# An encoder layer on one core: layer weights kept in two parts in DRAM for the second sequence, every second small part of the u tiles made anew by GpSimd

## The chip, the core and the metric

The kernel runs on 1 core of one Trainium2 chip, with its five engines: TensorE (PE; its weight loads are the row PEld), VectorE (DVE), ScalarE (ACT), GpSimd (POOL) and SyncE (SP), which here only issues DMAs. The metric is device time in microseconds of one execution. Three runs of the kernel before took 3474.37, 3475.89 and 3476.72 us; the median is 3475.89 us.

## The reference

One encoder layer (depth 1) is run on two sequences of 512 tokens with 1024 features, "prompt" and "sample", with the same weights. All is float32.

```
x = layer_norm(x)
h = x @ w_in                       # f_in 512, q 512, k 128, v 128, two gates of 1024
f = fft over tokens and group features of f_in, real part;  a = window attention(q, k, v)
x = layer_norm(2**0.25 * x + (sigmoid(g1) * (f @ w_fo) + sigmoid(g2) * (a @ w_ao)) @ w_out)
# PEER: 8 heads, 2 x 128 keys, the 16 best of 16384 experts for each token and head
eidx, gate = top16(x @ w_q, keys);  act = gelu(x . u[eidx])
cm  = sum(gate * act * v[eidx])
out = layer_norm(2**0.25 * x + cm + sigmoid(x @ ple_wg) * (p @ ple_wp))
```

## The kernel before

**Two parts.** A product that needs float32 accuracy is made of three TensorE matmuls (lines 1198 to 1200): large part by large part, large by small, small by large. The large part of a tile (w_hi) is a rounded copy that ScalarE makes (split_w, L464, for layer weights; split_u, L615, for u). The small part (w_lo for layer weights, u_lo for u) is raw minus large, on GpSimd, in two halves of 512 columns (split, L716).

**Tiles.** A layer has 69 weight tiles of 128x1024 (512 KB): 11 for the Fourier input, q, k and v, 24 for gates and merge (MERGE_AT), 8 for w_out (OUT_AT), 16 for w_q (QUERY_AT), 10 for the ple term (PLE_AT). Then come 128 u tiles. Each of these tiles is 24 matmuls with 512 columns. After the 128 u tiles of the sample come 128 v tiles (24 matmuls each), for the sample alone.

**Order.** Prompt: layer, u tiles (all expert activations, each tile of them stored to act_dram; VectorE chooses the experts beside it). Sample: layer, u tiles 0 to 61 (VectorE chooses, four choices of 128 tokens, and TensorE turns each choice at tiles CHOICE_AT = 16, 31, 46, 61), u tiles 62 to 125 with one batch of gates each (8 extra small matmuls, each in the trace as two, on one-hot tiles that VectorE makes, spread_batch), two more u tiles, then the v tiles.

**The prompt's experts.** The prompt's weighted sum over v goes by gather instead: 512 rows (4 token tiles by 128 choices), each an indirect DMA of 128x1024 from v into v_row (L767, 4 buffers) and an indirect DMA of 128 activations (L750, "value"), both issued by GpSimd in fetch_rows; VectorE adds each row into acc (L861) in add_rows. The rows are laid out over the whole sample part by fixed numbers: VectorE's are rows_before(j) at layer tile j, 2 at each of 10 gaps of a choice, 2 for each batch of gates, the rest over the v tiles (rows_at). A row can only be asked for when VectorE has taken the row four before (semaphore row_taken).

**Small parts of u.** In the prompt GpSimd makes all 128 and SyncE stores them to lo_dram; in the sample SyncE loads them back (u_lo_back), so GpSimd makes none. In the sample's layer GpSimd does both its 69 splits and rows, in the order that the loop over LAYER_TILES writes out: split of a tile, then the rows due. SyncE's queue loads weight j when the small part of tile j - 2 is made (load_w). In the v tiles VectorE makes the small parts.

## Time and profile before

| | |
|---|---|
| median of three runs | 3475.89 us |
| profiled execution | 3475.6 us, its span 3473.8 us |
| TensorE busy | 3240.2 us, 93% |
| VectorE busy | 1972.3 us, 57% |
| GpSimd busy | 2047.1 us, 59% |
| ScalarE busy | 1093.1 us, 31% |
| mean granted TensorE clock | 0.972 |
| GpSimd rows and values (L767, L750), 512 each | 691.9 us and 633.0 us |
| GpSimd splits of layer weights, 276 halves | 355.3 us |
| GpSimd splits of u, 256 halves | 362.1 us |

The profile is of one execution, and a busy TensorE is not one at its peak: matmuls overlap, so the number of matmuls in a stretch says more than the busy time. The chain of work that ended last has 67% of the span on TensorE and 17% on GpSimd. The shares of the page mix stages; a stage is read from the windows of the trace, and a wait by what ended it.

### The profile page before, as it was taken

The numbers are of one execution on the slowest core, as the hardware profiler recorded it, in microseconds if no ns is written. First come the engines' busy times: TensorE is split into PE (matmuls) and PEld (weight loads), VectorE is DVE, ScalarE is ACT, GpSimd is POOL, SyncE is SP. The second block draws the span as 40 slices with busy tenths as digits, with TensorE's granted clock in tenths as the row PEclk, the third lists the DMA queues.
The fourth block names the chain that finished last, engine by engine and source line by source line (L and its number), as shares of the span: only waits on it lengthen the run. The fifth ranks groups of instructions, "written<-read, shape, count | busy, mean of one in ns | idle before, by whom it ended". The sixth has DMA issues, their size and how long they took to land.

```text
span 3473.8 us, 40747 instructions
## 1 busy us (share of the span) xinstructions
PE 3240.2 (93%) x14740; PEld 2654.7 (76%) x14740; DVE 1972.3 (57%) x3363; ACT 1093.1 (31%) x1496; POOL 2047.1 (59%) x1568
## 2 busy tenths in 40 slices
PE   7999899999999999787889999999997999999997
PEld 6588787888888875566778888788886777777775
DVE  3511318992000007323437999788885877787778
ACT  2522223333222235211222333344453222222221
POOL 3044345565444474566476556577775888788883
PEclk9999899999999999888899999999998999999998
DMA  4022237777777853444349999899999999999995
GB/s 162 17 90 97 79 102 252 242 240 242 241 241 242 266 183 119 153 143 146 113 154 351 372 365 367 315 398 394 395 392 389 318 337 342 333 334 338 328 333 201
DMA packets 302660, 879.73 MB, mean 253 GB/s; under 512 B 44688, under 2 KB 77968, under 8 KB 299920
## 3 DMA queue, kind: packets, MB, share of 16 engines
q1 hardware_dynamic: 211216, 604.46, 49.9%
q0 software_dynamic: 91264, 272.96, 22.0%
q8 instruction: 103, 1.69, 0.2%
q14 instruction: 77, 0.63, 0.1%
HBM read 701.11 MB, written 176.16 MB: 253 GB/s over the span
## 4 chain that ended last, share of the span: by engine, by line
PE 67%; POOL 17%; issue 5%; DVE 5%; DMA 3%; ACT 1%; DVEq 1%; SPq 0%; POOLq 0%; ACTq 0%
PE ps L1198 20%; PE ps L1200 20%; PE ps L1199 20%; POOL value L750 8%; POOL v_row L767 8%; PE ps L1446 3%; DMA v_row<-in_v_rows,row_i 2%; POOL w_lo L716 1%; DVE acc L861 1%; PE ps L1376 1%; PE ps L1297 1%; DMA w_raw<-in_weights 1%; ACT probs L531 1%; PE ps L1339 0%; PE ps L1282 0%
## 5 line engine op out<-in xcount | busy, mean ns | idle before, releaser
L1198 PE MATMUL ps<-xt_hi,w_hi 128*128 128x512 f32 (+1 forms) x2800 | 1140.8, 407 | 63.9 <-POOL w_lo L716 53.1
L1199 PE MATMUL ps<-xt_lo,w_hi 128*128 128x512 f32 (+1 forms) x2800 | 1089.3, 389 | 0.0
L767 POOL DMA_INDIRECT v_row<-in_v_rows,row_i x512 | 691.9, 1351 | 502.2 <-DVE acc L861 396.7
L1200 PE MATMUL ps<-xt_hi,u_lo 128*128 128x512 f32 x2048 | 801.0, 391 | 0.0
L861 DVE SCALAR_TENSOR_TENSOR acc<-v_row,share,acc 128x1024 f32<-128x1024 f32 x512 | 663.1, 1295 | 190.9 <-DMA v_row<-in_v_rows,row_i 152.1
L750 POOL DMA_INDIRECT value<-act_dram,value_i x512 | 633.0, 1236 | 155.2 <-issue 154.9
L1198 PEld LDWEIGHTS ps<-xt_hi,w_hi 128*128 128x128 f32 x2800 | 537.0, 192 | 158.7 <-POOL w_lo L716 60.8
L1199 PEld LDWEIGHTS ps<-xt_lo,w_hi 128*128 128x128 f32 x2800 | 537.1, 192 | 84.2 <-issue 0.5
L716 POOL TENSOR_TENSOR w_lo<-w_raw,w_hi 128x512 fp32r<-128x512 f32 x276 | 355.3, 1310 | 388.6 <-ACT w_hi L464 387.6
L716 POOL TENSOR_TENSOR u_lo<-u_raw,w_hi 128x512 fp32r<-128x512 f32 x256 | 362.1, 1436 | 342.1 <-ACT w_hi L615 329.1
L1198 PE MATMUL ps<-w_hi,a_hi 128*128 128x512 f32 x1024 | 405.4, 396 | 61.0 <-DVE a_lo L1170 60.9
L634 ACT ACTIVATE act_t<-ps 128x512 f32<-128x512 f32 x256 | 153.1, 598 | 971.8 <-PE ps L1200 971.8
L1200 PEld LDWEIGHTS ps<-xt_hi,u_lo 128*128 128x128 f32 x2048 | 385.1, 188 | 82.3
L1200 PE MATMUL ps<-w_hi,a_lo 128*128 128x512 f32 x1024 | 403.2, 394 | 0.0
L1199 PE MATMUL ps<-u_lo,a_hi 128*128 128x512 f32 x1024 | 403.2, 394 | 0.0
L1200 PE MATMUL ps<-xt_hi,w_lo 128*128 128x512 f32 (+1 forms) x752 | 288.6, 384 | 0.0
L1198 PEld LDWEIGHTS ps<-w_hi,a_hi 128*128 128x128 f32 x1024 | 195.3, 191 | 111.6 <-DVE u_lo L1168 51.5
L615 ACT ACTIVATE w_hi<-u_raw 128x1024 fp32r<-128x1024 f32 x256 | 272.3, 1064 | 23.1 <-PE ps L1200 14.0
L827 DVE TENSOR_TENSOR xt_lo<-ps,xt_hi 128x512 fp32r<-128x512 f32 x32 | 20.4, 682 | 401.2 <-ACT xt_hi L474 401.2
L695 ACT ACTIVATE w_hi<-u_raw 128x1024 fp32r<-128x1024 f32 x128 | 135.6, 1059 | 336.0 <-PE ps L1200 335.9
L1446 PEld LDWEIGHTS ps<-hot_row,hot_col 128*128 128x128 f32 x1024 | 192.9, 188 | 44.9
L1200 PEld LDWEIGHTS ps<-w_hi,a_lo 128*128 128x128 f32 x1024 | 194.9, 190 | 41.3
(174 smaller groups left out, 3651.1 us busy)
## 6 DMA issues: line engine op xcount, KB each, us to landing
u_raw<-in_u_t SPq DMA_DIRECT2D x256, 512.0 KB, 6.4
w_raw<-in_weights SPq DMA_DIRECT2D x138, 512.0 KB, 3.3
lo_dram<-u_lo SPq DMA_DIRECT2D x128, 512.0 KB, 5.1
act_dram<-act_t SPq DMA_DIRECT2D x256, 256.0 KB, 5.2
u_lo<-lo_dram SPq DMA_DIRECT2D x128, 512.0 KB, 7.6
u_raw<-in_v_rows SPq DMA_DIRECT2D x128, 512.0 KB, 5.9
g_dram<-g_tile SPq DMA_DIRECT2D x16, 2048.0 KB, 13.2
act_in<-act_dram SPq DMA_DIRECT2D x128, 256.0 KB, 6.6
```

Of the source, the lines that this page charges most:

```text
L531: act.activation(probs[:, u % 2, h, 0:w], probs[:, u % 2, h, 0:w], ACT.Exp, bias=neg_max[:, u % 2, h:h + 1], accum_out=row_sum[:, u % 2, h ...
L615: act.activation(w_hi[:, (mu + n) % 2, :], u_raw[:, slot, :], ACT.Copy).then_inc(w_hi_made, 1)
L634: act.activation(act_t[:, slot, :], ps[:, n % 2, :], ACT.Gelu).then_inc(act_made, 1)
L695: act.activation(w_hi[:, n % 2, :], u_raw[:, n % DEEP, :], ACT.Copy).then_inc(v_hi_made, 1)
L716: pool.tensor_tensor(lo[:, here], raw[:, here], hi[:, here].bitcast(F32), ALU.subtract).then_inc(w_lo_made[half], 1)
L750: pool.indirect_dma_start(out=value[:, tt, k:k + 1], out_offset=None, in_=values, in_offset=bass.IndirectOffsetOnAxis(ap=value_i[:, tt, k: ...
L767: pool.indirect_dma_start(out=v_row[:, i % ROWS_DEEP, :], out_offset=None, in_=v_rows, in_offset=bass.IndirectOffsetOnAxis(ap=row_i[:, tt, ...
L861: dve.scalar_tensor_tensor(out=there, in0=v_row[:, i % ROWS_DEEP, :], scalar=share[:, tt, k:k + 1], in1=there, op0=ALU.mult, op1=ALU.add). ...
L1198: pe.matmul(where, lh, rh, start=first, stop=False)
L1199: pe.matmul(where, lh, rl, start=False, stop=False)
L1200: return pe.matmul(where, ll, rh, start=False, stop=last)
L1446: mm = pe.matmul(ps[:, 4 + 2 * (batch % 2) + k // 4, cols_of(k % 4)], hot_col[:, batch % 2, k, :], hot_row[:, batch % 2, k, :], start=True ...
```

## The change

Four things change.

1. **Pairs.** In the prompt's layer SyncE stores both parts of each tile to pair_dram (keep_w, 1 MB for each of 69 tiles, in two DMAs, queued behind the load of the tile two later). ScalarE may overwrite w_hi only once the tile is stored (w_kept). In the sample's layer SyncE loads both parts as one 1 MB DMA into one of three slots (load_pair), when TensorE has used the tile three before; ScalarE's and GpSimd's splits of the sample's layer are gone, and TensorE waits for pair_in.
2. **u tiles.** Only the small parts of even u tiles are stored in the prompt and loaded in the sample (64 of 128). In the sample GpSimd makes those of odd tiles (MADE), between the rows.
3. **Rows.** GpSimd asks first for 18 values, then rows_at_tile(n) rows ahead of the split of odd tile n. VectorE takes 10 rows before the first scores of the sample's attention, 16 in it, then 7 for every 4 layer tiles. By the end of the sample's layer 125 rows are due instead of 75; the choices (80) and batches (128) keep theirs, and the v tiles have 179 instead of 229.
4. **Loops.** TensorE's loops of the sample's layer are written out, since three slots don't fit a loop of two.

```diff
-LAYER_ROWS = 7
+START_ROWS, UNIT_ROWS = 10, 2
-FIRST_VALUES = 3
+FIRST_VALUES = 18
+PAIRS = 3
 def rows_before(j):
-    return j + LAYER_ROWS
+    return START_ROWS + UNITS * UNIT_ROWS + 7 * (j - MERGE_AT) // 4
+def reloaded(n):
+    return n % 2 == 0
+def rows_at_tile(n):
+    gates = n - GATES_AT
+    return ROWS_LAYER + GAPS * GAP_ROWS * NT * n // GATES_AT if gates < 0 else rows_at_batch(min(gates, GATE_BATCHES))
...
+        pair = at("pair", 42, [P, PAIRS, 2, D], F32R)
...
+            def keep_w(m):
+                slot = m % 2
+                sp.dma_start(pair_dram[m, :, 0, :], w_hi[:, slot, :].bitcast(F32)).then_inc(w_kept[slot], 16)
+                sp.dma_start(pair_dram[m, :, 1, :], w_lo[:, slot, :].bitcast(F32)).then_inc(w_kept[slot], 16)
+            def load_pair(j):
+                sp.dma_start(pair[:, j % PAIRS].bitcast(F32), pair_dram[j]).then_inc(pair_in[j % PAIRS], 16)
             def load_layer(s, first, last):
                 for j in range(first, last):
-                    load_w(s * STREAM + j, (s * STREAM + j) % 2, weights[j])
+                    if s:
+                        sp.wait_ge(w_used, made(STREAM + j - PAIRS))
+                        load_pair(j)
+                    else:
+                        load_w(j, j % 2, weights[j])
+                        if j >= 2:
+                            keep_w(j - 2)
...
                 if s == 0:
+                    for j in (LAYER_TILES - 2, LAYER_TILES - 1):
+                        sp.wait_ge(w_lo_made[1], made(j))
+                        keep_w(j)
...
-                        sp.dma_start(lo_dram[n], u_lo[n % DEEP][:].bitcast(F32)).then_inc(u_lo_stored[n % DEEP], 16)
+                        if reloaded(n):
+                            sp.dma_start(lo_dram[n], u_lo[n % DEEP][:].bitcast(F32)).then_inc(u_lo_stored[n % DEEP], 16)
...
                     for n in range(EXPERT_TILES):
-                        sp.wait_ge(w_hi_made, mu + n + 1)
+                        sp.wait_ge(w_hi_made, STREAM + n + 1)
+                        if not reloaded(n):
+                            sp.wait_ge(w_lo_made[1], 2 + STREAM + made_upto(n))
...
             def split_w(s, m, slot):
-                act.wait_ge(w_in[slot], landed(m - s * EXPERT_TILES, slot))
+                if s:
+                    return
+                act.wait_ge(w_in[slot], landed(m, slot))
+                act.wait_ge(w_kept[slot], 16 * (m - slot) + 16)
                 act.wait_ge(w_used, slot_free(m))
...
+                    if s == 0 and n < 2:
+                        for kept in range(2):
+                            act.wait_ge(w_kept[kept], 16 + 32 * len(range(kept, LAYER_TILES, 2)))
                     act.activation(w_hi[:, (mu + n) % 2, :], u_raw[:, slot, :], ACT.Copy).then_inc(w_hi_made, 1)
...
-            for j in range(LAYER_TILES):
-                m = STREAM + j
...
-                split_w(m, m % 2)
...
-                fetch_rows(rows_fetched(j))
+            for _ in range(FIRST_VALUES):
+                fetch_value()
+            pool.wait_ge(resid_stored, 16 * NT)
+            for tt in range(2):
+                fetch_acc(tt)
+            for n in MADE:
+                m = STREAM + LAYER_TILES + n
+                fetch_rows(rows_at_tile(n))
+                pool.wait_ge(w_hi_made, STREAM + n + 1)
+                split(u_lo[n % DEEP][:], w_hi[:, m % 2, :], u_raw[:, n % DEEP, :])
             fetch_rows(GATHERS)
...
+                if s:
+                    add_rows(START_ROWS)
                 dve.wait_ge(mix_in, 32 * (s + 1))
...
+            def arrived(s, m, half):
+                if s:
+                    pe.wait_ge(pair_in[(m - STREAM) % PAIRS], 16 * ((m - STREAM) // PAIRS + 1))
+                else:
+                    pe.wait_ge(w_lo_made[half], made(m))
...
-                pe.wait_ge(u_lo_back[slot], 16 * (n // DEEP + 1))
+                if reloaded(n):
+                    pe.wait_ge(u_lo_back[slot], 16 * (kept_before(n) + 1))
+                else:
+                    for half in range(2):
+                        pe.wait_ge(w_lo_made[half], 2 + STREAM + made_upto(n))
```

The order of GpSimd's instructions in the sample's layer, before (w_lo is the small part of a layer weight, v_row a gathered row, value a gathered activation; "waits" names semaphores):

```order
L716 TENSOR_TENSOR w_lo<-w_raw,w_hi 128x512 [waits w_hi_made]
L716 TENSOR_TENSOR w_lo<-w_raw,w_hi 128x512
L767 DMA v_row<-in_v_rows,row_i 128x1024 [waits row_taken]
L750 DMA value<-act_dram,value_i 128x1
L716 TENSOR_TENSOR w_lo<-w_raw,w_hi 128x512 [waits w_hi_made]
L716 TENSOR_TENSOR w_lo<-w_raw,w_hi 128x512
```

and now, from the last u tile of the prompt (u_lo_68 to u_lo_71 are the four slots of small parts) into the sample's layer:

```order
L778 TENSOR_TENSOR u_lo_70<-u_raw,w_hi 128x512
L778 TENSOR_TENSOR u_lo_71<-u_raw,w_hi 128x512 [waits w_hi_made]
L778 TENSOR_TENSOR u_lo_71<-u_raw,w_hi 128x512
L812 DMA value<-act_dram,value_i 128x1 [waits act_stored3,act_stored2,row_i_made,act_stored1,act_stored0]
L812 DMA value<-act_dram,value_i 128x1 x17
L798 DMA acc<-resid_dram 128x1024 [waits resid_stored]
L798 DMA acc<-resid_dram 128x1024
L829 DMA v_row<-in_v_rows,row_i 128x1024
L812 DMA value<-act_dram,value_i 128x1
```

The two halves of a split no longer stand behind a row that waits for row_taken; only values and rows are left there.

GpSimd at the end of the sample's layer and the start of the choices, before:

```order
L767 DMA v_row<-in_v_rows,row_i 128x1024 [waits row_taken]
L750 DMA value<-act_dram,value_i 128x1
L716 TENSOR_TENSOR w_lo<-w_raw,w_hi 128x512 [waits w_hi_made]
L716 TENSOR_TENSOR w_lo<-w_raw,w_hi 128x512
L767 DMA v_row<-in_v_rows,row_i 128x1024 [waits row_taken]
L750 DMA value<-act_dram,value_i 128x1
L767 DMA v_row<-in_v_rows,row_i 128x1024 [waits row_taken]
L750 DMA value<-act_dram,value_i 128x1
```

and now, at a place in the batches of gates:

```order
L829 DMA v_row<-in_v_rows,row_i 128x1024 [waits row_taken]
L812 DMA value<-act_dram,value_i 128x1
L829 DMA v_row<-in_v_rows,row_i 128x1024 [waits row_taken]
L812 DMA value<-act_dram,value_i 128x1
L829 DMA v_row<-in_v_rows,row_i 128x1024 [waits row_taken]
L812 DMA value<-act_dram,value_i 128x1
L829 DMA v_row<-in_v_rows,row_i 128x1024 [waits row_taken]
L812 DMA value<-act_dram,value_i 128x1
L778 TENSOR_TENSOR u_lo_71<-u_raw,w_hi 128x512 [waits w_hi_made]
L778 TENSOR_TENSOR u_lo_71<-u_raw,w_hi 128x512
```

Where only rows and values stood, four rows with their values and the two halves of one odd u tile alternate; the split stands behind rows that wait for row_taken.

SyncE's queue in the prompt's layer, before:

```order
L359 DMA resid_71<-in_x 128x1024 x3
L316 DMA w_raw<-in_weights 128x1024 [waits w_lo_made1] x8
L369 DMA gdft<-in_group_dft 128x256
L370 DMA bias<-in_attn_bias 128x3072
L316 DMA w_raw<-in_weights 128x1024 [waits w_lo_made1] x3
```

and now:

```order
L398 DMA resid_72<-in_x 128x1024 x3
L341 DMA w_raw<-in_weights 128x1024 [waits w_lo_made1] x3
L345 DMA pair_dram<-w_hi 128x1024
L346 DMA pair_dram<-w_lo 128x1024
L341 DMA w_raw<-in_weights 128x1024 [waits w_lo_made1]
L345 DMA pair_dram<-w_hi 128x1024
L346 DMA pair_dram<-w_lo 128x1024
```

Two stores of 512 KB stand between any two weight loads of the prompt.

## Rows read from the trace of the kernel before

**Rows 1.** One call for the stages; us, busy us by engine (instructions), clock, DMA share, GB/s.

```profile
176.00:358.00 182.00, 175.69 (x771) 143.73 (x769) 33.85 (x54) 49.59 (x62) 81.22 (x64) 0.99 0.30 100
358.00:532.00 174.00, 164.48 (x831) 140.81 (x832) 37.39 (x52) 45.73 (x56) 67.90 (x52) 0.95 0.25 83
900.00:1200.00 300.00, 300.00 (x1325) 248.39 (x1325) 0.00 (x0) 85.68 (x111) 139.65 (x111) 1.00 0.78 248
1236.00:1306.00 70.00, 65.89 (x343) 54.77 (x342) 7.00 (x12) 22.53 (x32) 53.88 (x50) 1.00 0.57 199
...
1390.00:1651.00 261.00, 202.36 (x770) 161.40 (x768) 83.30 (x96) 53.75 (x70) 157.66 (x133) 0.86 0.44 148
1651.00:1845.00 194.00, 168.61 (x833) 143.72 (x834) 70.60 (x79) 45.73 (x56) 118.34 (x102) 0.92 0.46 150
1845.00:2189.00 344.00, 339.03 (x1501) 280.44 (x1500) 323.38 (x929) 114.08 (x145) 200.87 (x161) 1.00 0.99 368
2189.00:2690.00 501.00, 482.88 (x2609) 413.67 (x2609) 395.51 (x336) 225.67 (x264) 344.27 (x258) 0.98 0.99 382
2300.00:2350.00 50.00, 50.00 (x276) 42.92 (x274) 42.58 (x37) 23.95 (x28) 38.36 (x28) 1.00 1.02 390
2690.00:3447.00 757.00, 713.92 (x3069) 582.32 (x3070) 603.72 (x638) 210.50 (x256) 591.47 (x434) 0.98 0.93 326
```

**Rows 2.** Waits, 1392 to 1660 us; waiter <- waited for: us in total, times, longest.

```profile
PE ps L1198 <- POOL w_lo L716: 52.1, 10, 10.1
...
POOL v_row L767 <- DVE acc L861: 66.4, 10, 9.2
```

**Rows 3.** Timeline of GpSimd, 1450 to 1485 us; start, duration, instruction, idle before it.

```profile
1463.79 2.54 POOL L716 TENSOR_TENSOR w_lo<-w_raw,w_hi 128x512 fp32r<-128x512 f32 x2 [1.87 <-ACT w_hi L464]
1472.70 1.93 POOL L767 DMA_INDIRECT v_row<-in_v_rows,row_i  x1 [6.38 <-DVE acc L861]
```

**Rows 4.** DMA issues, 1400 to 1640 us; KB each, median us to landing.

```profile
w_raw<-in_weights SPq DMA_DIRECT2D x31, 512.0 KB, 3.4
...
v_row<-in_v_rows,row_i POOLq DMA_INDIRECT x33, 5.3
```

**Rows 5.** DMA issues, 2700 to 3400 us.

```profile
u_raw<-in_v_rows SPq DMA_DIRECT2D x118, 512.0 KB, 5.8
...
v_row<-in_v_rows,row_i POOLq DMA_INDIRECT x210, 7.4
```

**Rows 6.** DMA issues of the whole page.

```profile
lo_dram<-u_lo SPq DMA_DIRECT2D x128, 512.0 KB, 5.1
```

**Rows 7.** Timeline of ScalarE, 515 to 560 us.

```profile
527.26 1.06 ACT L615 ACTIVATE w_hi<-u_raw 128x1024 fp32r<-128x1024 f32 x1 [4.38 <-PE ps L1200]
```

**Rows 8.** Groups of GpSimd, 1850 to 2150 us; shapes xcount, busy, mean ns, idle.

```profile
L767 POOL DMA_INDIRECT v_row<-in_v_rows,row_i x74 | 104.0, 1405 | 103.7 <-DVE acc L861 91.5 <-issue 12.2
L750 POOL DMA_INDIRECT value<-act_dram,value_i x73 | 80.0, 1096 | 22.3 <-issue 22.3
```

**Rows 9.** Timeline of TensorE, 2145 to 2195 us.

```profile
2188.67 0.77 PE L1198 MATMUL ps<-xt_hi,w_hi 128*128 128x512 f32 x1 [4.97 <-DVE hot_row L1151]
```

**Rows 10.** Groups of GpSimd and VectorE, 2210 to 2650 us.

```profile
L767 POOL DMA_INDIRECT v_row<-in_v_rows,row_i x120 | 164.4, 1370 | 78.5 <-DVE acc L861 59.0 <-issue 19.5
L750 POOL DMA_INDIRECT value<-act_dram,value_i x121 | 160.7, 1328 | 36.9 <-issue 36.9
...
L861 DVE SCALAR_TENSOR_TENSOR acc<-v_row,share,acc 128x1024 f32<-128x1024 f32 x120 | 154.2, 1285 | 33.5 <-DMA v_row<-in_v_rows,row_i 23.1 <-issue 0.9
...
L1149 DVE TENSOR_TENSOR hot_col<-all_t,iota 128x1024 f32<-128x1024 f32 x60 | 73.2, 1221 | 0.0
```

**Rows 11.** Line 716, 640 to 660 us; duration ns min/median/max.

```profile
L716 POOL TENSOR_TENSOR u_lo<-u_raw,w_hi x8: 1278/2172/3349, 638.9 to 658.4; 128x512 fp32r<-128x512 f32 x8
```

**Rows 12.** Tile a_hi on TensorE; idle before it by releaser.

```profile
  DVE a_lo L1170: 60.9, 24
```

**Rows 13.** Waits, 2700 to 3440 us.

```profile
DVE acc L861 <- DMA v_row<-in_v_rows,row_i: 120.3, 80, 5.6
```

More of the change, by code:

```diff
@@ L105, in rows_at_choice, with kept_before, made_upto @@
     return ROWS_LAYER + GAPS * GAP_ROWS * (tt + 1)
+RELOADED = [n for n in range(EXPERT_TILES) if reloaded(n)]
+MADE = [n for n in range(EXPERT_TILES) if not reloaded(n)]
+def kept_before(n):
+    return len([m for m in RELOADED if m < n and m % DEEP == n % DEEP])
+def made_upto(n):
+    return len([m for m in MADE if m <= n])
+def rows_at_tile(n):
+    gates = n - GATES_AT
+    return ROWS_LAYER + GAPS * GAP_ROWS * NT * n // GATES_AT if gates < 0 else rows_at_batch(min(gates, GATE_BATCHES))
 def rows_at_batch(batch):
@@ L250, in encoder @@
         w_used = sem("w_used")
+        w_kept, pair_in = [sem(f"w_kept{k}") for k in range(2)], [sem(f"pair_in{k}") for k in range(PAIRS)]
         u_lo_stored, u_lo_back = ([sem(f"{n}{k}") for k in range(DEEP)] for n in ("u_lo_stored", "u_lo_back"))
@@ L363, in _ @@
                 else:
[L364 removed]
+                    load_layer(s, PAIRS, 8)
                     sp.wait_ge(w_lo_made[1], made(base - 1))
@@ new lines, in _ @@
+                    sp.wait_ge(w_used, made(mu + EXPERT_TILES - DEEP + 1))
+                    for slot in range(2):
+                        sp.wait_ge(w_kept[slot], 16 + 32 * len(range(slot, LAYER_TILES, 2)))
+                    load_pair(0)
+                    sp.wait_ge(w_used, made(mu + EXPERT_TILES - 1))
+                    load_pair(1)
+                    for k in range(2, DEEP):
+                        if kept_before(EXPERT_TILES + k):
+                            sp.wait_ge(u_lo_stored[k], 16 * kept_before(EXPERT_TILES + k))
@@ L1217, in rows, with half_columns @@
                         mm = three(ps[:, bank + tt, :], act_hi[:, k0 + k, cols_of(tt)], act_lo[:, k0 + k, cols_of(tt)],
-                                   w_hi[:, slot, w], w_lo[:, slot, w], first and k == 0, last and k == 1)
+                                   large(s, m, m % 2)[:, w], small(s, m, m % 2)[:, w], first and k == 0, last and k == 1)
                 return mm
-            def half_columns(where, m, act_hi, act_lo, half):
+            def half_columns(where, s, m, act_hi, act_lo, half):
                 t = slice(half * T // 2, (half + 1) * T // 2)
@@ L1225, in half_columns, with turn @@
                     if k % (KD // 2) == 0:
-                        pe.wait_ge(w_lo_made[k // (KD // 2)], made(m))
+                        arrived(s, m, k // (KD // 2))
                     w = slice(k * P, (k + 1) * P)
-                    mm = three(where[:, t], w_hi[:, m % 2, w], w_lo[:, m % 2, w], act_hi[:, k, t], act_lo[:, k, t], k == 0, k == KD - 1)
+                    mm = three(where[:, t], large(s, m, m % 2)[:, w], small(s, m, m % 2)[:, w], act_hi[:, k, t], act_lo[:, k, t], k == 0, k == KD - 1)
                 return mm
-            def turn(nth, norm, m, where):
+            def turn(nth, norm, s, m, where):
                 for tt in range(NT):
@@ L1383, in _, with two_sides @@
                 key_scores(0, 1)
[L1384 to L1388 removed]
+                def two_sides(n):
+                    query(n, 1)
+                    key_scores(n, 0)
+                    query(n + 2, 0)
+                    key_scores(n, 1)
+                if s == 0:
+                    with pe.Fori(1, SIDES // 2 - 1) as i:
+                        two_sides(2 * i)
+                else:
+                    for n in range(2, SIDES - 2, 2):
+                        two_sides(n)
                 query(SIDES - 2, 1)
```

153 lines of the change are left out of this document (75 added, 78 removed).

## The prediction

> **What bounds the kernel now.** I read first the page's shares and slices, then the windows of the stages, then in each stage the waits and the groups of the engine named there. TensorE sets the pace. At full pace it starts 1325 matmuls in 300 us, 0.2264 us each, so a tile of 24 takes 5.43 us [rows 1]. Against that pace the sample loses time in four places.
>
> - Layer, gates to w_out: 261 us for 770 matmuls. The prompt does the same work, 771 matmuls, in 182 us [rows 1]. The excess is 79 us. Here TensorE waited 52.1 us, in 10 waits of up to 10.1 us, for GpSimd's w_lo, and GpSimd waited 66.4 us for VectorE to take a row [rows 2]. Both come from one queue: the split of a tile stands behind a row that VectorE will take only after the merge that TensorE has not finished. The timeline has it: split, 6.38 us of waiting for VectorE, the next row [rows 3].
> - Layer, norm to ple: 194 us against 174 in the prompt, 20 us more [rows 1].
> - End of the choices: TensorE stands 4.97 us for VectorE's one-hot tiles [rows 9]. VectorE is busy 323 of 344 us there [rows 1], so it binds as closely as TensorE.
> - v tiles: 757 us, where 3072 matmuls by 0.2264 are 695. TensorE was idle 60.9 us for VectorE's a_lo [rows 12], VectorE 120.3 us for rows that had not landed [rows 13], and GpSimd was busy 591 of 757 us [rows 1] and has 0.3 us between any two gathers beside that.
>
> In the gates TensorE has no such loss: in 2300 to 2350 us it is busy throughout, with 276 matmuls [rows 1]. A tile there has 24 and, as recorded, 16 small ones, so 40 in 7.27 us.
>
> **The change part by part**, against the profiled execution: span 3473.8 us and 1.8 us around it, 3475.6 us. The median of the runs is 3475.89 us, 0.3 us more, so I use the one for the other.
>
> *Prompt.* 69 MB more are written. By the window 176 to 358 us the layer's DMA share is 0.30 at 100 GB/s, while 900 to 1200 us moves 248 GB/s at 0.78 [rows 1]; 1 MB more in 5.43 us is 193 GB/s, so 293 GB/s and a share near 0.92. A store of 512 KB lands in 5.1 us [rows 6], a weight load in 3.4 [rows 4]; queued in one line, load and two stores take some 7 us. They start 3.6 us after the tile four back is used (ScalarE's 1.06 us [rows 7], two halves in 2.54 [rows 3]) and must end by 10.9 us, which they do by a hair, with 3 us more until TensorE would feel it. Behind the last tile the cover is gone: split_u(0), now at 527.26 us [rows 7], waits for the last keep_w. The split of the last layer tile ran one tile earlier, near 521.8, its small part was made at 525.5, its two stores land near 532, and the sigmoid stands behind it on ScalarE. I take +3.5 us; bounds 0 and +12 (a 1 us stall at each eighth tile on top).
>
> *Turn, Fourier tiles and attention.* TensorE was busy 65.9 of 70 us from 1236 to 1306 [rows 1]: splits and waits for raw weights go (-4), pair 0 is asked for only when the last u tile's activation is stored (+1). The 10 rows that VectorE takes before the first scores cost 18 values and 10 rows on GpSimd, some 50 us, inside these 70. I take -3; bounds -4 and +8.
>
> *Layer, gates to w_out.* The waits for w_lo cannot occur. What is late next is rows and pairs. VectorE takes 5.25 rows for each merge of three tiles (16.3 us): 5.25 by 1.285 is 6.7 us, the merge about 4, and the fifth and sixth row, asked for as the first are taken, land 5.3 us [rows 4] to 7.4 us [rows 5] later, so a merge's period is 14 to 17 us. GpSimd needs 1.75 rows of at most 3.10 us (the price beside the choices, below), 5.4 us of 5.43, and less while VectorE is idler. A pair has 10.9 us to land; 512 KB take 5.8 us at 326 GB/s [rows 1, 5], and here 1.9 MB for each tile are 350 GB/s, so 8 to 10 us. Of the 79 us I keep 8: -71; bounds -79 and -50.
>
> *Layer, norm to ple.* Same reasoning, of 20 us I keep 7 (the rows of two groups of four w_out tiles stand ahead of the norm on VectorE): -13; bounds -20 and 0.
>
> *Choices.* 31 splits are added on GpSimd. A row with its value costs 1.405 + 1.096 + 2 by 0.3, 3.10 us [rows 8]; for two tiles that is 2.58 by 3.10, 8.0 us, and a split between its 2.54 alone [rows 3] and the 4.4 beside dense work (below); I take 3.2, since less than half of VectorE's work here reads two tiles (80 rows are 103 of 323 us). In all 11.2 of 10.9 us. The 91.5 us in which GpSimd waited for VectorE [rows 8] are the cover, and 31 by 3.2 uses it up. Queued behind the split's wait for w_hi are the rows, for these waits VectorE, for it TensorE at tile 61. VectorE also loses where a split holds it off, some 31 by 0.6. As VectorE is already the last to arrive, all of this shows: +28; bounds +5 and +55.
>
> *Gates.* The term that decides. Two tiles take 14.5 us. GpSimd has four rows, 4 by (1.370 + 1.328 + 0.6), 13.2 us [rows 10], and now one split as well. Two halves take 2.6 us with VectorE nearly idle [rows 3]. VectorE here works 395 of 501 us [rows 1], nearly all in instructions of 1.2 to 1.3 us that read two tiles [rows 10]. The nearest rows are 8 halves beside such instructions in the prompt's choice, median 2.17 us [rows 11]: 4.4 for a split. With a slower period VectorE works less densely, which gives back some 0.5. 13.2 + 4.4 - 0.5 is 17.1 us, so 32 by 2.6, +82; I take +80. Bounds: rows at the price of the choices and a free split, 4 by 3.10 + 2.6 = 15.0 us, +15; the longest half of [rows 11], 3.35, once in each split with a free one is 4.6, and the rows unchanged, 17.8 us, +107.
>
> The Trainium skill (SBUF — State Buffer, Who interferes with whom) has it that a VectorE instruction with two SBUF inputs contends with a GpSimd one that reads SBUF, and that the pair of ports is held for a whole instruction. This case's trace agrees: halves of 1.27 us alone, up to 3.35 beside such work. By that rule each half would wait a full instruction of 1.22 us, a split would be 5.0 us, and the gates +117.
>
> *v tiles.* 179 rows in place of 229: 1.40 a tile by (1.36 + 1.36 + 0.6, as in the gates about 3.3) is 4.6 of 5.43 us, where it was 1.79 by 3.3, 5.9 (which the lags of other engines spread out). So GpSimd keeps four rows ahead, and VectorE's 603.7 us for 128 tiles [rows 1] go from 4.7 to 4.2 a tile. Of 61 us I keep 9: -52; bounds -35 and -61. The tail stays.
>
> Sum: 3.5 - 3 - 71 - 13 + 28 + 80 - 52 = -27.5 us, so **3448 us**.
>
> **Rivals.**
> - *GpSimd is not the limit in the u tiles* (the wait for VectorE between rows is a soft one, and splits slip into it). For it: from 2210 to 2650 us GpSimd still waited 59.0 us for VectorE [rows 10], 1.8 us for each split, and a row asked for just after that wait is one of the dear ones. Against it: that is less than a split. Choices +8, gates +15: 3448 - 85 = 3363 us.
> - *The splits cost more than the layer gives back*, the other side. Place: GpSimd between u tiles 62 and 125, where splits, held off by VectorE's two-input instructions, stand behind rows, and where each half holds VectorE off in turn. It decides from a period of 18.0 us for two tiles on (+108 where I have +80). For it: the rows of the prompt's choice [rows 11] and the skill's rule above. By the rule alone the time is 3448 + 37 = 3485 us. At 18.5 us (+128, 5.8 us for a split and its effect on the rows) with the choices at +45 it is 3448 + 48 + 17 = 3513 us.
> - *DMA binds the sample's layer*: three slots of 1 MB and bursts of rows. In a burst a period holds 3 MB of pairs and 2.6 MB of rows, 5.6 MB in 16.3 us or 345 GB/s; the most that a stage here kept up is 382 GB/s at a share of 0.99 [rows 1]. For it: the margin is 10%. Against it: buffers of two tiles. It would leave the merges at 205 us and the rest at 190: 3448 + 15 + 9 = 3472 us.
> - *The change does not do what it says*: the splits of the sample's layer are gone from the order, so this one is out.
>
> **How the numbers follow.** My forecast has 0.44, its own range 3425 to 3475. GpSimd not the limit has 0.24, about 3335 to 3395. The dear splits have 0.22, 3480 to 3545. The DMA has 0.10. This kernel's measurement tells a change from none at about 0.2%, 7 us, so no change is 3469 to 3483 us. Faster: 0.37 of the forecast's, all of the cheap one's, 0.02 of the DMA's, 0.63. The same: 0.06, 0.01 and 0.03, 0.10. Slower: the rest, 0.27. The range that leaves out half of the cheap case and a third of the dear one is 3360 to 3515 us.
>
> **What would show it.** Right: no split of w_lo after 1236 us; merges and w_out of the sample in 185 to 195 us; two u tiles with gates in 16.5 to 17.5 us with GpSimd busy over 85% and TensorE waiting for u_lo or hot_row; halves of line 716's successor at 2 us or more there; v tiles near 705 us. Wrong: gates still near 7.3 us a tile (first rival); TensorE waiting for pair_in in the merges (DMA); a stage of gates above 600 us (second rival); rows not landed that still hold the v tiles at 740 us.

## The result, and the profile after

The changed kernel takes 3696.1 us (median of 4 runs, 3691.7 to 3705.2) where the kernel before takes 3475.8: the ratio is 1.064, 95% interval 1.0615 to 1.0660. It is 6.4% slower; I had forecast 3448 us, and the time lies above the range (3360 to 3515 us) too. The profiled execution has a span of 3697.7 us, 223.9 more than the 3473.8 of before. The stages below are read from one profiled execution of each kernel, the times are medians.

Five marks in the traces divide a span: TensorE's first transpose of the sample's input, ScalarE's last sigmoid of the layer, TensorE's first gate matmul (hot_row), and the first and last matmul of the v tiles.

| stage, us | before | after | difference | forecast |
|---|---|---|---|---|
| prompt | 1237.0 | 1249.9 | +12.9 | +3.5 |
| sample's layer | 603.6 | 568.2 | -35.4 | -87 |
| choices | 349.5 | 438.0 | +88.5 | +28 |
| gates | 499.7 | 716.2 | +216.5 | +80 |
| v tiles | 757.3 | 698.7 | -58.6 | -52 |
| tail | 26.7 | 26.7 | 0 | 0 |

The layer, in the parts of the forecast: the turn, Fourier tiles and attention (153 us in before, to the first merge at 1390 us) take 203, +50 for a forecast of -3; merges and w_out (1453 to 1640 us) take 187 in place of 261, -74 for -71; norm to ple takes 178 in place of 190, -12 for -13.

The windows of after that answer to [rows 1] (window, length, busy us by engine with instructions, granted clock, DMA share, GB/s):

```profile
1250.00:1260.00 10.00, 7.42 (x61) 6.88 (x62) 3.83 (x7) 3.79 (x7) 5.50 (x6) 1.00 0.90 343
...
1290.00:1300.00 10.00, 1.49 (x4) 1.13 (x4) 4.98 (x4) 0.00 (x0) 7.86 (x8) 0.50 0.59 186
...
1320.00:1330.00 10.00, 10.00 (x40) 8.11 (x40) 0.00 (x0) 0.60 (x1) 0.00 (x0) 0.87 0.73 284
1818.00:2256.00 438.00, 363.39 (x1523) 294.66 (x1523) 349.29 (x931) 115.88 (x147) 291.25 (x226) 0.91 0.74 255
2256.00:2972.00 716.00, 521.11 (x2606) 441.58 (x2604) 415.79 (x334) 222.41 (x264) 398.67 (x329) 0.86 0.71 246
...
2972.00:3671.00 699.00, 698.71 (x3070) 577.99 (x3071) 547.03 (x586) 202.09 (x257) 507.33 (x333) 1.00 0.91 316
```

In the v tiles TensorE is busy for all of 699 us: a_lo holds it up once, for 21.8 us before the first of them, where it was 60.9 us in 24 waits [rows 12]. In the gates no engine is near its limit. TensorE works 521 of 716 us, VectorE 416, and GpSimd, which I had called the bound, 399: 56%. It is no engine's throughput; it is a loop of waits. The waits of after, 2250 to 2960 us (waiter <- waited for: us in total, times, longest):

```profile
POOL u_lo L778 <- ACT w_hi L675: 245.2, 32, 18.8
DVE acc L916 <- DMA v_row<-in_v_rows,row_i: 223.0, 35, 15.9
PEld ps L1255 <- issue: 181.0, 19, 12.4
PE ps L1255 <- DVE hot_row L1208: 174.3, 17, 12.2
```

One turn of the loop, from the timelines of the four engines (start, duration, instruction, in brackets the idle time before it and what ended it):

```profile
2505.42 1.08 ACT L675 ACTIVATE w_hi<-u_raw 128x1024 fp32r<-128x1024 f32 x1
2506.59 2.75 POOL L778 TENSOR_TENSOR u_lo<-u_raw,w_hi 128x512 fp32r<-128x512 f32 x2 [11.30 <-ACT w_hi L675]
2509.49 0.95 POOL L829 DMA_INDIRECT v_row<-in_v_rows,row_i  x1 [0.15 <-issue]
...
2512.00 0.94 POOL L829 DMA_INDIRECT v_row<-in_v_rows,row_i  x1 [0.30 <-issue]
...
2514.96 1.28 DVE L916 SCALAR_TENSOR_TENSOR acc<-v_row,share,acc 128x1024 f32<-128x1024 f32 x1 [8.01 <-DMA v_row<-in_v_rows,row_i]
...
2523.10 1.51 DVE L916 SCALAR_TENSOR_TENSOR acc<-v_row,share,acc 128x1024 f32<-128x1024 f32 x1 [6.85 <-DMA v_row<-in_v_rows,row_i]
2524.53 2.28 DVE L1205 TENSOR_TENSOR hot_row<-all_t,iota 128x1024 f32<-128x1024 f32 x1
2526.73 1.21 DVE L1206 TENSOR_TENSOR hot_col<-all_t,iota 128x1024 f32<-128x1024 f32 x1
2528.02 1.23 DVE L1208 TENSOR_TENSOR hot_row<-hot_row,all_t 128x1024 f32<-128x1024 f32 x1
2529.50 0.76 PE L1255 MATMUL ps<-xt_hi,w_hi 128*128 128x512 f32 x1 [11.58 <-DVE hot_row L1208]
```

Read it backwards. TensorE stands 11.58 us for the one-hot tile of VectorE. VectorE was late because it must first add two rows, and the second, asked for at 2512.00, held it until 2523.10. GpSimd had not asked sooner, since its whole queue of rows stood behind the split, and the split stood 11.30 us for ScalarE's w_hi. ScalarE may make that w_hi only when TensorE has used the tile two earlier. So each link waits for the one before it, and TensorE's own delay comes round again as GpSimd's wait.

A full turn is longer than these lines. TensorE's stop before this one ended at 2487.02 us, so from start to start are 42.5 us, in which it uses four tiles; four take 29.0 at pace. The first 18.4 us go from TensorE's start to w_hi at 2505.42 (two tiles and ScalarE's work behind them), the other 24.1 are the chain above. TensorE so stops for hot_row 17 times among the 64 tiles, 174.3 us in all. Each stop also costs clock: from 2487 to 2490 us the granted clock is 0.52, the lower level, and the first two groups of five matmuls (two of the five are halves of a gate matmul) take 1.70 and 1.45 us where the later ones take 0.92, 1.3 us lost; behind the stop shown it is 2.2 us. Over 17 stops that is, as an estimate, 22 to 37 us. With the waits it makes up most of the 216.5.

The choices have the same loop at the four tiles where TensorE transposes VectorE's choice: it waits 41.9 us there (4 times, up to 14.7), and GpSimd then up to 15.3 us for w_hi. That is the route that I had written down for the choices (the rows behind the split's wait, VectorE behind them, TensorE at tile 61) and priced as a difference of throughputs.

The layer came out 52 us short of its forecast, nearly all of it in its first part and for a reason that no term held. From 1264 to 1313 us TensorE crawls, with nothing named. Its timeline in after:

```profile
1290.59 0.37 PE L1256 MATMUL ps<-xt_lo,pair 128*128 128x256 f32 x1 [2.43 <-issue]
1293.41 0.37 PE L1257 MATMUL ps<-xt_hi,pair 128*128 128x256 f32 x1 [2.45 <-issue]
1295.54 0.37 PE L1255 MATMUL ps<-xt_hi,pair 128*128 128x256 f32 x1 [1.76 <-issue]
1298.34 0.37 PE L1256 MATMUL ps<-xt_lo,pair 128*128 128x256 f32 x1 [2.43 <-issue]
```

The pair that it reads has landed, GpSimd issues its values and rows beside it, and the profile names no engine or transfer as what ended the idle times. The windows above show the same: 4 matmuls in 10 us at a clock of 0.50, which is the lower of its two levels (1.2 GHz), then 40 in 10 us from 1320 on.

### The profile page after: what moved, and what is told of

Its sections match the earlier page's. It is cut to its first block, busy times and chain, and to the rows that moved or that the text cites. A ratio compares the mean times of both kernels' runs of the same rounds, so it can differ in the third digit from the quotient of the medians.

```text
span 3697.7 us, 40588 instructions
## 1 busy us (share of the span) xinstructions
PE 3270.6 (88%) x14740; PEld 2676.2 (72%) x14740; DVE 2017.2 (55%) x3363; ACT 1016.9 (28%) x1427; POOL 2041.2 (55%) x1558
## 3 DMA queue, kind: packets, MB, share of 16 engines
q0 software_dynamic: 91264, 272.96, 21.8%
## 4 chain that ended last, share of the span: by engine, by line
PE 58%; issue 13%; DVE 9%; POOL 7%; DMA 7%; DVEq 2%; ACT 2%; another core or an unknown queue 2%; SPq 0%; POOLq 0%; ACTq 0%
PE ps L1255 18%; PE ps L1256 18%; PE ps L1257 18%; DMA v_row<-in_v_rows,row_i 5%; POOL w_lo L778 4%; DVE acc L916 3%; POOL u_lo L778 2%; PE ps L1542 2%; ACT g_tile L725 1%; DVEq L1207 1%; POOL value L812 1%; POOL v_row L829 1%; DVE hot_row L1208 1%; PE ps L1374 1%
## 5 line engine op out<-in xcount | busy, mean ns | idle before, releaser
L1255 PE MATMUL ps<-xt_hi,w_hi 128*128 128x512 f32 (+1 forms) x2424 | 1010.2, 417 | 215.9 <-DVE hot_row L1208 174.3
L1256 PE MATMUL ps<-xt_lo,w_hi 128*128 128x512 f32 (+1 forms) x2424 | 956.6, 395 | 0.0
L778 POOL TENSOR_TENSOR u_lo<-u_raw,w_hi 128x512 fp32r<-128x512 f32 x384 | 558.7, 1476 | 676.8 <-ACT w_hi L675 667.5
L916 DVE SCALAR_TENSOR_TENSOR acc<-v_row,share,acc 128x1024 f32<-128x1024 f32 x512 | 679.4, 1327 | 446.3 <-DMA v_row<-in_v_rows,row_i 358.0
L829 POOL DMA_INDIRECT v_row<-in_v_rows,row_i x512 | 668.5, 1306 | 416.3 <-DVE acc L916 288.8
L1257 PE MATMUL ps<-xt_hi,u_lo 128*128 128x512 f32 x2048 | 815.5, 398 | 0.0
L1255 PEld LDWEIGHTS ps<-xt_hi,w_hi 128*128 128x128 f32 x2424 | 469.9, 194 | 303.8 <-issue 208.8
L1256 PEld LDWEIGHTS ps<-xt_lo,w_hi 128*128 128x128 f32 x2424 | 470.0, 194 | 71.9 <-issue 0.2
L1255 PE MATMUL ps<-w_hi,a_hi 128*128 128x512 f32 x1024 | 399.7, 390 | 21.8 <-DVE a_lo L1227 21.8
L778 POOL TENSOR_TENSOR w_lo<-w_raw,w_hi 128x512 fp32r<-128x512 f32 x138 | 180.7, 1330 | 356.5 <-ACT w_hi L520 356.5
L1225 DVE TENSOR_TENSOR u_lo<-u_raw,w_hi 128x1024 fp32r<-128x1024 f32 x128 | 156.8, 1225 | 133.6 <-ACT w_hi L757 90.4
```

What stands on the lines that cost most here:

```text
L778: pool.tensor_tensor(lo[:, here], raw[:, here], hi[:, here].bitcast(F32), ALU.subtract).then_inc(w_lo_made[half], 1)
L829: pool.indirect_dma_start(out=v_row[:, i % ROWS_DEEP, :], out_offset=None, in_=v_rows, in_offset=bass.IndirectOffsetOnAxis(ap=row_i[:, tt, ...
L916: dve.scalar_tensor_tensor(out=there, in0=v_row[:, i % ROWS_DEEP, :], scalar=share[:, tt, k:k + 1], in1=there, op0=ALU.mult, op1=ALU.add). ...
L1225: dve.tensor_tensor(v_lo[n % 2][:], v_raw[:, slot, :], v_hi[:, n % 2, :].bitcast(F32), ALU.subtract).then_inc(v_lo_made, 1)
L1255: pe.matmul(where, lh, rh, start=first, stop=False)
L1256: pe.matmul(where, lh, rl, start=False, stop=False)
```

## The experiments

Each time is the median of 4 to 10 executions, each ratio is to the kernel before in the same session, with its 95% interval. A stage's length comes from the marks above, in one profiled execution.

**All small parts reloaded** (the changed kernel without the splits among the u tiles).

```diff
 def reloaded(n):
-    return n % 2 == 0
+    return True
```

> The changed kernel with the small parts of all 128 u tiles stored and loaded back; GpSimd makes none in the sample. Both theories on the u tiles (a row's chain is queued behind a split that waits for TensorE; GpSimd has too much work beside VectorE) expect choices and gates back at about 845 us from the 1120 of the changed kernel, the v tiles still near 699 us, so 3697 - 275 = 3420 us, below the kernel before. The slow issue of TensorE near 1264 to 1313 us (50 us) stays if code, pairs or GpSimd's unbroken DMAs make it. If the pairs themselves cost, it stays above 3476 us.

Measured: 3398.4 us, ratio 0.977 (0.974 to 0.980), so 2.3% faster than before. The choices take 352.8 us and the gates 498.8, as before (349.5 and 499.7); the layer 565.5 and the v tiles 698.6, as after. The splits made anew cost the whole 298 us between the two, and the rest of the change is a gain. The prompt, though, takes 1255.6 us here, where it was 1249.9 in after.

**Only the splits, without pairs** (the kernel before, with odd u tiles made anew on GpSimd, rows asked for at the old rates).

```diff
+            for n in MADE:
+                m = STREAM + LAYER_TILES + n
+                fetch_rows(max(rows_at_tile(n), rows_asked))
+                pool.wait_ge(w_hi_made, m + 1)
+                split(u_lo[n % DEEP][:], w_hi[:, m % 2, :], u_raw[:, n % DEEP, :])
```

> The kernel before with one part of the change alone: odd u tiles are made by GpSimd between the rows in the sample, layer weights as before, rows as before. Either theory on the u tiles expects most of the loss here, the u tiles at 1050 to 1120 us instead of 845: 3680 to 3750 us, and no slow issue of TensorE near the start of the sample.

Measured: 3777.3 us, ratio 1.086 (1.084 to 1.089). Gates 719.9 us and choices 429.9, that is +220 and +80, with the same waits (GpSimd 236.6 us in 32 for w_hi). Prompt 1237.9, layer 603.8, v tiles 755.6: unchanged. TensorE's slow issue is absent. Both large losses come from this part alone.

**Rows asked for one split earlier** (the changed kernel, same instructions in another order).

```diff
             for n in MADE:
-                fetch_rows(rows_at_tile(n))
+                fetch_rows(rows_at_tile(n + 2))
                 pool.wait_ge(w_hi_made, STREAM + n + 1)
```

> The changed kernel with the rows of the next odd u tile asked for ahead of each split, one period earlier; all work the same. If the loss is a chain (PE used -> w_hi -> split -> rows -> landing -> VectorE -> one-hot tiles -> PE), the gates fall from 10.6 us a tile to 8 to 9, the u tiles from 1120 us to 900 to 980, the time to 3480 to 3560 us. If GpSimd's work or the port is what binds, nothing moves: 3680 to 3700 us.

Measured: 3491.8 us, ratio 1.004 (1.003 to 1.005), 204 us less by one changed number. Gates 545.2 us, choices 401.1. The groups of GpSimd from 2300 to 2700 us, first in after, then here (shapes xcount | busy, mean ns | idle before, releaser):

```profile
L829 POOL DMA_INDIRECT v_row<-in_v_rows,row_i x75 | 84.5, 1127 | 19.9 <-issue 19.1
L778 POOL TENSOR_TENSOR u_lo<-u_raw,w_hi 128x512 fp32r<-128x512 f32 x38 | 59.7, 1592 | 128.1 <-ACT w_hi L675 128.1
```

```profile
L829 POOL DMA_INDIRECT v_row<-in_v_rows,row_i x100 | 125.5, 1255 | 28.3 <-issue 24.1 <-DVE acc L916 2.2
L778 POOL TENSOR_TENSOR u_lo<-u_raw,w_hi 128x512 fp32r<-128x512 f32 x50 | 93.2, 1883 | 4.5 <-ACT w_hi L675 4.1
```

The wait for w_hi falls from 128.1 to 4.1 us in a window of 400, though each half of a split is dearer here (1.88 us against 1.59). The splits cannot be the cause where they are cheaper. What is left in the gates, 45.5 us over before, is 1.4 us for each of 32 periods, and GpSimd is busy 430 of 545 us. Of the 51.6 us that the choices keep the trace names two parts: TensorE waits 21.5 us (10 times) for a small part of GpSimd's and 12.9 us (3 times) for VectorE's choice. In the gates it waits 20.7 us (14 times) for ScalarE's copies of gates. These come from the made splits too, but how was not tried.

**The split cut to a sixteenth** (the changed kernel; from the fifth u tile on, a made tile's small part is renewed in 32 of 512 columns of each half, the others keep an older tile's).

```diff
-                split(u_lo[n % DEEP][:], w_hi[:, m % 2, :], u_raw[:, n % DEEP, :])
+                split(u_lo[n % DEEP][:], w_hi[:, m % 2, :], u_raw[:, n % DEEP, :], T if n < DEEP else 32)
```

> Base: the changed kernel (3696 us; choices 438, gates 716 us). From the fifth u tile on, the split of a made tile covers 32 of the 512 columns of each half, some 0.3 us in place of 2.5 to 3.7; the rest of its small part stays that of an older tile. Waits, order and number of instructions are the same. Theory of the prediction (GpSimd's throughput sets the gates: 13.2 us of rows and 4.4 of split for two tiles): without the split it has 14 us, the gates fall to about 505 us and the choices to about 360, together 3400 to 3440 us. Theory of the loop (GpSimd waits for w_hi with the rows queued behind, and every link of the loop counts once): the period of 22.4 us loses only the split's 2.5 to 3.7 us, so the gates take 600 to 640 us, the choices 410 to 430, together 3580 to 3610 us.

Measured: 3609.8 us, ratio 1.038 (1.036 to 1.039), where throughput alone would give 3440 at most. Choices 409.5 us, gates 660.4. The loop's expectation (3580 to 3610 us) holds for the whole, at its very edge; the gates are 20 us above its range and the choices at its lower end. A half takes 0.43 us in place of 1.59, so a split 2.3 us less, and a period of the gates falls by 55.8 / 32 = 1.7 us. The waiting is all still there:

```profile
L829 POOL DMA_INDIRECT v_row<-in_v_rows,row_i x81 | 101.1, 1248 | 25.1 <-issue 18.7 <-DVE acc L916 4.5
L812 POOL DMA_INDIRECT value<-act_dram,value_i x80 | 91.4, 1143 | 24.4 <-issue 24.4
L778 POOL TENSOR_TENSOR u_lo<-u_raw,w_hi 128x32 fp32r<-128x32 f32 x42 | 17.1, 427 | 148.1 <-ACT w_hi L675 148.1
```

Of the 216.5 us that the gates lost, 55.8 go with the split's work and 171.0 with the place of the rows. Together that is 10 us more than was lost, so the two overlap by at least that.

**TensorE's loops written out** (the kernel before; the three loops of the sample's layer as straight code, for the slow issue).

```diff
-                with pe.Fori(0, KD // 2) as i:
-                    for j in range(2):
-                        merge(2 * i, j)
+                for n in range(KD):
+                    merge(n - n % 2, n % 2)
```

> The kernel before with TensorE's loops of the sample's layer written out, all else as before. If written-out code makes TensorE's slow issue of 50 us at the turn, it appears here: 3520 us or more. If pairs or GpSimd's DMAs make it, this kernel takes what the one before takes, 3470 to 3480 us.

Measured: 3479.0 us, ratio 1.0005 (0.9993 to 1.0016). No slow issue; straight code by itself costs nothing here.

**GpSimd started later** (all small parts reloaded; its 18 values wait for the ninth tile).

```diff
             pool.wait_ge(row_i_made, NT)
+            pool.wait_ge(w_used, made(STREAM + 8))
             for _ in range(FIRST_VALUES):
```

> Base: the version that reloads all small parts (3398 us), in which TensorE issues one instruction in 0.7 to 1.4 us from 1272 to 1321 us. Here GpSimd starts its 18 values only when TensorE has used the ninth tile of the sample. Theory A, the slow issue comes from GpSimd's unbroken run of indirect DMAs beside the turn: the turn is free of it, the ninth tile comes some 30 us sooner; the values and ten rows then delay VectorE's first scores by up to 45 us, and the slow issue may come back beside them, so the time is 3365 to 3400 us. Theory B, it comes from the 3 MB of pairs or from the pairs' own instructions: the slow stretch stands where it was, GpSimd's work comes on top of it, 3420 to 3450 us.

Measured: 3387.3 us, ratio 0.974 (0.971 to 0.976). The turn is free of it, and the slow stretch has moved with the values, which now start at 1310.18 us. How much of what follows 1320 us is slow issue can't be told, since TensorE also waits there for other engines (8.1 us for pq, 8.6 for probs). Windows of this kernel:

```profile
1270.00:1280.00 10.00, 10.00 (x50) 8.46 (x49) 0.00 (x0) 1.20 (x2) 0.00 (x0) 1.00 0.71 274
...
1310.00:1320.00 10.00, 10.00 (x46) 8.26 (x45) 0.00 (x0) 1.76 (x3) 7.69 (x8) 1.00 1.04 397
1320.00:1330.00 10.00, 5.33 (x25) 4.36 (x23) 0.00 (x0) 0.60 (x1) 7.56 (x9) 0.99 0.49 182
1330.00:1340.00 10.00, 5.80 (x12) 3.52 (x12) 0.90 (x2) 1.79 (x3) 7.86 (x10) 0.50 0.57 186
```

**Three values a tile** (the same base; each three wait for one more used tile).

```diff
-            for _ in range(FIRST_VALUES):
+            for k in range(FIRST_VALUES):
+                if k % 3 == 0:
+                    pool.wait_ge(w_used, made(STREAM + k // 3))
                 fetch_value()
```

> Base: the version that reloads all small parts (3398 us). The 18 values are asked for three at a time, the next three when TensorE has used one more tile; the rows follow as before. Theory A (the unbroken run of indirect DMAs slows TensorE's issue): the slow stretch goes or shrinks to the time of the rows, 3350 to 3380 us. Theory B (pairs): 3395 to 3405 us.

Measured: 3360.7 us, ratio 0.965 (0.962 to 0.968), as the first theory had it. TensorE is busy 66.6 us of the 70 from 1250 to 1320, and the layer takes 525.9 us in place of 565.5. It now waits 9.8 us for the first probs.

**The values in one run in the kernel before** (no pairs).

```diff
-                if j < 6:
-                    for _ in range(FIRST_VALUES):
+                if j == 0:
+                    for _ in range(6 * FIRST_VALUES):
                         fetch_value()
```

> Base: the kernel before (3476 us), without pairs. All 18 values of the sample's start are asked for in one run behind the first split, in place of three with each of six tiles. Theory A (the unbroken run slows TensorE's issue): a stretch in which TensorE's matmuls stand 0.7 us or more apart with nothing else named, beginning some 12 us after the first value, and 3485 to 3520 us. Theory B (pairs): no such stretch, the splits of two to four tiles come up to 20 us late, 3476 to 3496 us.

**The same with two small products of constants behind each value.**

```diff
                         fetch_value()
+                        for _ in range(2):
+                            pool.drain()
+                            pool.tensor_tensor(scratch[:], ident[:], iota[:], ALU.mult)
```

> Base: the kernel before with its 18 values in one run (3497.6 us; TensorE idle 19.5 us with nothing named, from 1248 to 1268 us). Behind each value GpSimd now does two small products of constants, so that its indirect DMAs stand some 2.2 us apart in place of 1.25, over some 40 us. Theory C (GpSimd issuing back to back keeps TensorE's instructions from arriving): the gap of 19.5 us goes, TensorE waits for w_lo of tile 1 instead, up to 25 us, which shows as a wait for GpSimd and not for the issue. Theory D (the count of indirect DMAs in a row or their descriptors does it, whatever their distance): the gap without a name stays or grows to 30 us or more. The time says little between the two; the name of the wait tells.

Measured: 3497.6 us, ratio 1.005 (1.003 to 1.007), and 3541.0 us, 1.018 (1.017 to 1.020). Neither tells anything of the slow issue, and this is how a trace misleads. In the first TensorE is idle 19.48 us "<-issue" until 1267.85, which looked like the first theory's gap. But GpSimd's split of tile 1, behind the values, starts at 1266.52, and its first half ends some 1.26 us later, at 1267.78, just as TensorE goes on: the wait is for w_lo. The second names it (66.0 us for w_lo). The values stood 3.8 us apart there, not the 2.2 that I had expected. A TensorE that has nothing it may do cannot show a slow issue, and the base was the wrong one. It was wrong in a second way: TensorE's code there is the loops of before and not straight code.

**The values 5 us apart** (the right base: all small parts reloaded, the same place, nothing tied to TensorE).

```diff
             for _ in range(FIRST_VALUES):
                 fetch_value()
+                pool.drain()
+                pool.tensor_tensor(scratch[:], ident[:], iota[:], ALU.mult)
```

> Base: the version that reloads all small parts (3398 us; TensorE's slow issue from 1272 to 1321 us, beside 18 values that stand 1.25 us apart and then rows and values). GpSimd starts its 18 values at the same place, tied to nothing of TensorE, but does one small product of constants behind each, so that they stand some 2.7 us apart; the rows and values behind them follow 1.25 us apart as before. Theory C (GpSimd's indirect DMAs back to back keep TensorE's instructions from arriving): no slow issue in the first 45 us, perhaps some beside the rows, 3350 to 3380 us, and blocks of instructions land in this stretch. Theory D (their number in a row does it, whatever their distance): the slow issue starts some 12 to 25 us after the first value and lasts as long as the run, 3395 to 3430 us.

Measured: 3394.4 us, ratio 0.975 (0.972 to 0.979), above my 3380: the 18 values stood 3.2 to 9.4 us apart, some 5 on average, not 2.7, and TensorE later waited 46.4 us for VectorE's probs, which needs them. The question is answered all the same:

```profile
1270.00:1280.00 10.00, 10.00 (x45) 8.26 (x44) 0.00 (x0) 1.17 (x2) 2.90 (x4) 1.00 0.69 258
1280.00:1290.00 10.00, 10.00 (x46) 8.28 (x45) 0.00 (x0) 1.20 (x2) 2.89 (x4) 1.00 0.54 191
1290.00:1300.00 10.00, 10.00 (x46) 8.29 (x45) 0.00 (x0) 1.20 (x2) 2.89 (x4) 1.00 0.88 345
1300.00:1310.00 10.00, 10.00 (x46) 8.29 (x45) 0.00 (x0) 1.78 (x3) 1.45 (x2) 1.00 0.72 259
```

Same pairs, same straight code, same values from the same moment on, and TensorE at full pace for 60 us. So the slow issue needs GpSimd's indirect DMAs close together; pairs and straight code without that do not make it. Whether it needs the pairs or the straight code as well is not shown. The rows behind the values did follow 1.36 us apart, but TensorE stood for probs then and could show nothing.

**The large part stored first** (the version with three values a tile; in the prompt's layer).

```diff
+                        if j >= 2:
+                            keep_hi(j - 2)     # as soon as w_hi is made
                         load_w(j, j % 2, weights[j])
                         if j >= 2:
-                            keep_w(j - 2)
+                            keep_lo(j - 2)
```

> Base: the paced version (3360.7 us; its sample starts at 1253.4 us where the kernel before has 1237.0). In the prompt's layer the store of a tile's large part goes into the queue as soon as ScalarE has made it, ahead of the next weight load, and only the small part's store stands behind that load. Theory A (the prompt's 16 us are ScalarE's waits for the two stores, 91 us in 34 waits, of which part shows on TensorE): the sample starts 5 to 14 us sooner, 3347 to 3356 us. Theory B (the prompt is bound by the bytes): no change, 3358 to 3363 us.

**Fewer rows before the first scores** (on top of that).

```diff
-START_ROWS, UNIT_ROWS = 10, 2
+START_ROWS, UNIT_ROWS = 2, 2
-NORM_PROMPT_AT = 4
+NORM_PROMPT_AT = 12
```

> Base: the version with the large part stored first, sent along with this one. VectorE takes 2 rows in place of 10 before the sample's first scores, and the eight are taken in the v tiles; the first prompt norm moves from u tile 4 to 12. Theory A (TensorE's wait of 9.8 us for the first probs is VectorE's and GpSimd's ten rows): that wait shrinks under 4 us, and the time is 6 to 10 us under the base. Theory B (the attention is bound by its own chain, and the v tiles have no room): within 3 us of the base.

Measured: 3348.3 us, ratio 0.963 (0.961 to 0.964), and 3334.7 us, 0.958 (0.957 to 0.960). The first brings the sample's start from 1253.4 to 1241.6 us (from one execution each; the second starts it at 1243.5, and with the old order it lies between 1249.8 and 1255.6, so the gain is 6 to 14 us): the waits of ScalarE for the stores' end, 150 to 560 us, fall from 90.9 us in 34 to

```profile
ACT w_hi L527 <- DMA pair_dram<-w_lo: 34.3, 14, 5.9
```

The second takes the wait for the first probs away, 11.0 us in hi_first, and the v tiles keep their 697.7 us with eight rows more. Its layer takes 516.5 us, 87.1 less than before, which is what I had forecast for the pairs. This is the best kernel of the study, 4.2% faster than the one before.

## Why the prediction was wrong

*The step that failed* is the gates' term (and in the same way that of the choices): "13.2 + 4.4 - 0.5 is 17.1 us, so 32 by 2.6", four rows and one split on GpSimd for two tiles. It made a period from the sum of one engine's work. I had written in the term of the choices what is queued behind the split's wait, but took the wait itself as free, as if the split could run whenever GpSimd had time. It can't: w_hi(n) comes late in the period, because ScalarE makes it when tile n-2 is used, and the rows for VectorE's next batch stand behind it, two per batch, 11.1 us from asking to landing for the second in the turn shown. Four links in a line (ScalarE's w_hi 1.2, the split 2.8, then 13.8 until the second row has landed, VectorE 6.4) are 24.1 us from w_hi to TensorE's next start. With the 18.4 us before them the loop takes 42.5 us for four tiles, 21.2 for two, where I had 17.1. The mean agrees: the 499.7 us of before are 32 periods of 14.5 and 36 us outside them, and (716.2 - 36) / 32 = 21.3 us. Measured +216.5 for my +80, and +88.5 for +28, both above their bounds (+107 and +55). Asking a period ahead shows the same work at 545.2 us, +45.5, under my own figure.

*The price of a split* was too high: 2 by 1.59 = 3.2 us in after and 2 by 1.88 = 3.8 with dense work, for my 4.4. These rows lie between 2.54 us alone [rows 3] and the 5.0 that I had by the rule. The Trainium skill (SBUF — State Buffer, Who interferes with whom) has whoever issues second wait until the other is done, so a full instruction of 1.22 us is the most that a half can wait, and I had taken it as the rule. If a half starts at any moment of VectorE's work, it waits on average half an instruction, 0.61 us, for the share of the time in which VectorE is busy (416 of 716 us in after, 447 of 545 with the rows ahead): an estimate of 1.62 and 1.77 us, where 1.59 and 1.88 were measured. The traces agree with the rule read this way. The rival of the dear splits named this side and this place, and its sign (gates above 600 us) came, but for the wrong reason, and its 3513 us was far below as well. (Its threshold has a slip: 18.0 us for two tiles are 32 by 3.46, +111 and not +108.) "GpSimd is not the limit" was true in the literal sense and wrong in what I made of it, a faster kernel.

*The layer*: merges to ple were right in mechanism and size (-86 for -84). What failed is the turn, +50 for -3. With values three at a time the layer is -77.7, with two early rows as well -87.1, which meets my -87 for a kernel with ten rows and is in part luck. Missing was the slow issue, about 40 us (565.5 to 525.9 us), and with it the ten early rows, 9.4 us. I had the 18 values and 10 rows on GpSimd "inside these 70" and looked only at who waits for them. DMA did not bind: TensorE waited 2.4 us for pairs in the start.

*The prompt*: +12.9 for +3.5, just outside the bound of 12. In the six other kernels that store their pairs in this order it is +12.8 to +18.6. "By a hair" was the warning: two stores and a load in one line. ScalarE waited 90.2 us in 30 waits for the second store, and 9.5 us more before split_u(0), where I had seen the cover end. A small part of each wait came through.

*The v tiles*: right. Fewer rows let GpSimd keep ahead, -58.6 for -52.

In sum the errors are +9.4, +51.6, +60.5, +136.5 and -6.6, together 251.4 us: 3699.5 in place of 3448, the 3697.7 us of the span and the 1.8 around it.

## What to carry to other kernels

Before a step that waits is put into an engine's queue, follow a full turn: what it waits for, what stands behind it, who needs that, and whether that one feeds the first wait. If the way closes, the period is the sum of the links and not the load of the busiest engine; put the urgent work ahead of the wait by a whole period, and only then count throughput. Where a cover fits by a hair over sixty tiles, price it as lost in part. A run of indirect DMAs from GpSimd 1.25 us apart is not free for the others only because nobody waits for it. And before a gap in some event is called a cause, count the work between two events: a slow engine makes such a gap by itself.

## What the hardware did that I had not expected

TensorE's issue slowed to one instruction (matmul or weight load) in 0.7 to 1.4 us beside GpSimd's indirect DMAs 1.25 us apart. The DMA queues seem to show why. Queue q8 carries blocks of 16 KB of instructions, one in 20 to 32 us where TensorE runs at pace. From 1261 to 1327 us after has none, while the version with three values a tile has three:

```profile
q0 software_dynamic: 3170, 8.41, 41.9%
q1 hardware_dynamic: 288, 2.10, 8.0%
```

```profile
q1 hardware_dynamic: 2808, 13.83, 55.1%
q0 software_dynamic: 2179, 5.07, 20.8%
q8 instruction: 3, 0.05, 0.3%
```

In the version with GpSimd started later the last block lands between 1308 and 1312 us, the first value is asked for at 1310.18, and the next block comes between 1384 and 1388. The Trainium skill (Runtime: NRT & Kernel Launch, Instruction fetch mechanics) has each engine fetch instructions through a DMA queue of its own, in blocks of 16 KiB. The size agrees with q8's.

Counted by work, there is no gap. In after a block lands between 1259 and 1260 us and the next between 1330 and 1331; from 1258 to 1330 us TensorE starts 129 matmuls and 128 weight loads. From 1202 to 1230 and from 1230 to 1258, between the blocks before, it starts 125 and 129 matmuls. In the version with GpSimd started later it starts 119 from 1310 to 1386. And in after TensorE goes on at one matmul in 0.43 us from 1318.67, some 12 us before the next block lands. So it was not short of a block: fewer came because it used fewer, and these stretches say nothing against the Trainium skill's statement, there too, that the fetch is mostly hidden. What slows the issue stays open.

A long run without pause is not enough either. In the v tiles of before, where TensorE's code is straight too, GpSimd issues 184 indirect DMAs with pauses of less than 0.5 us from 2724 to 3028 us, 1.65 us apart, and TensorE starts 1233 matmuls from 2724 to 3024 us, where full pace is 1325. In the slow stretch of after 18 stand 1.24 us apart and 28 more 1.33. With three values a tile the rows and last values ran some 40 us nearly back to back as well (1297 to 1338 us, with a few pauses of 0.6 to 0.9 us), and TensorE kept its pace of 46 matmuls in 10 us up to 1320. How long or how dense a run must be was not tried.
